# Tensor-engine experts without a loop, the last two experts interleaved, second-norm statistics on the scalar engine

## The reference, cut to what matters

```python
x1 = layer_norm(DEEPNORM_ALPHA * x + mix, ln1_g, ln1_b)
ffn = moe_ffn(x1, w_router, b_router, w_gate, b_gate, w_up, b_up, w_down, b_down)
x2 = layer_norm(DEEPNORM_ALPHA * x1 + ffn, ln2_g, ln2_b)

def expert_block(args):
    xe, e = args
    h = clamped_swiglu(xe @ w_gate[e] + b_gate[e], xe @ w_up[e] + b_up[e])
    return h @ w_down[e] + b_down[e]
```

## Time and profile before

| | us |
|---|---|
| Median of 3 runs (1635.64 to 1644.28) | 1637.16 |
| The profiled execution, whole time | 1636.67 |
| The profiled execution, span of the core | 1634.5 |
| PE busy in the span | 1492.2 |
| DVE, ACT, POOL busy | 388.5, 308.9, 113.5 |
| Mean traffic of the DMA engines | 287 GB/s |

### The profile page before, as it was taken

How to read it: one execution, slowest core, us unless ns; L and a number is a source line. 1 busy time by engine, 2 the same in 40 slices (tenths; PEclk the granted TensorE clock), 3 DMA queues, 4 the chain that set the end, 5 groups by cost and what they waited for, 6 DMA issues and landing times.

```text
span 1634.5 us, 38821 instructions
## 1 busy us (share of the span) xinstructions
PE 1492.2 (91%) x17456; PEld 1029.1 (63%) x17456; DVE 388.5 (24%) x620; ACT 308.9 (19%) x561; POOL 113.5 (7%) x123
## 2 busy tenths in 40 slices
PE   6999799887689989998998999899999989999991
PEld 6767697665656656665665666566566656666660
DVE  3422664535621111111111111111111111111104
ACT  4335332120121121111111111111111111121111
POOL 2002000000010000000001000000000000000000
PEclk8999555788589999999999999999999999999996
DMA  9322000032989999999999999999999999999923
GB/s 299 108 78 82 1 1 0 5 110 104 365 301 385 391 392 346 375 388 355 370 392 392 358 365 394 351 373 391 393 356 368 392 356 373 391 391 387 390 77 120
DMA packets 128644, 468.48 MB, mean 287 GB/s; under 512 B 11409, under 2 KB 12673, under 8 KB 128321
## 3 DMA queue, kind: packets, MB, share of 16 engines
q1 hardware_dynamic: 117648, 429.01, 67.9%
q0 software_dynamic: 10832, 36.89, 8.7%
HBM read 445.19 MB, written 22.76 MB: 286 GB/s over the span
## 4 chain that ended last, share of the span: by engine, by line
PE 82%; PEld 6%; issue 5%; DVE 4%; DMA 2%; ACT 1%; PEldq 0%; DVEq 0%; SPq 0%; ACTq 0%; POOLq 0%
PE unit L977 38%; PE unit L980 24%; PE unit L797 3%; PE unit L960 2%; PEld unit L632 2%; PEld unit L634 2%; PEld unit L633 2%; PE unit L965 2%; PE unit L994 2%; PE unit L761 1%; PE unit L784 1%; PE unit L632 1%; PE unit L930 1%; PE unit L633 1%; PE unit L634 1%
## 5 line engine op out<-in xcount | busy, mean ns | idle before, releaser
L980 PE MATMUL unit<-ring_a,xeT 128*32 128x256 f32 x1584 | 360.1, 387 | 0.0
L977 PE MATMUL unit<-ring_a,xeT 128*32 128x512 f32 (+1 forms) x3168 | 359.3, 496 | 0.0
L980 PE MATMUL unit<-ring_b,xeT 128*32 128x256 f32 x1488 | 329.1, 379 | 0.0
L977 PE MATMUL unit<-ring_b,xeT 128*32 128x256 f32 (+1 forms) x2976 | 328.2, 486 | 0.0
L980 PEld LDWEIGHTS unit<-ring_a,xeT 128*32 128x32 f32 x1584 | 176.5, 112 | 58.5 <-issue 4.5
L980 PEld LDWEIGHTS unit<-ring_b,xeT 128*32 128x32 f32 x1488 | 162.3, 110 | 52.6
L980 PE MATMUL unit<-ring_b,heT 128*32 128x256 f32 x816 | 181.0, 382 | 0.0
L977 PE MATMUL unit<-ring_b,heT 128*32 128x512 f32 (+1 forms) x1632 | 180.5, 490 | 0.0
L977 PEld LDWEIGHTS unit<-ring_a,xeT 128*32 128x32 f32 x3168 | 124.8, 112 | 72.5 <-issue 10.9
L980 PE MATMUL unit<-ring_a,heT 128*32 128x256 f32 x720 | 157.9, 379 | 0.0
L977 PE MATMUL unit<-ring_a,heT 128*32 128x256 f32 (+1 forms) x1440 | 157.5, 485 | 0.0
(11 more groups left out here) (292 smaller groups left out, 1620.3 us busy)
## 6 DMA issues: line engine op xcount, KB each, us to landing
ring_a<-w_gate_dram SPq DMA_DIRECT2D x68, 1024.0 KB, 9.0
ring_b<-w_down_dram SPq DMA_DIRECT2D x68, 1024.0 KB, 11.8
ring_a<-w_up_dram SPq DMA_DIRECT2D x64, 1024.0 KB, 10.9
ring_b<-w_up_dram SPq DMA_DIRECT2D x64, 1024.0 KB, 9.2
ring_b<-w_gate_dram SPq DMA_DIRECT2D x60, 1024.0 KB, 11.3
ring_a<-w_down_dram SPq DMA_DIRECT2D x60, 1024.0 KB, 10.4
raw_a<-w_in_dram SPq DMA_DIRECT2D x16, 512.0 KB, 4.8
raw_a<-w_out_dram SPq DMA_DIRECT2D x8, 512.0 KB, 3.4
```

The source lines that it names most:

```text
L977: return mm(out[j * NS:(j + 1) * NS, a:b], stat(j), w[:, a:b], start=False, stop=last)
L980: return mm(out[CAP:P, j * 256:(j + 1) * 256], stat(j), w[:, FOLD:D], start=False, stop=stop)
```

## The change

On PE the loop is gone: `pe_step` is written out for e from 0 to 30, and every wait for a chunk is against a constant. The other engines keep their loops.

For the last two experts PE's order is new. After the gate of expert 31 come up of 31, chunks 0 and 1 of down of 30, the transposes of h of 31, chunks 2 and 3 of down of 30, and down of 31 (`last_two`). SP requests the chunks in that order. The second h goes to a tile of its own, `heT_last`, which lies where the rows of even experts were, and the down product of 31 goes to `pg`. ACT copies h of 31 before it writes out expert 30. The numbers of instructions, chunks and bytes are those of before.

In the second norm DVE keeps the statistics of tile 0. Those of tiles 1 to 4 go to ACT: a pass that sums the row (Identity with an accumulator), the mean and its negative (two small Copies), a pass that sums the squares of the differences (Square with an accumulator), then the root. DVE then finishes one tile after the other.

```diff
 
         here[0] = phase_at
         xeT = sb("xeT", [P, 2, KD, CAP])
+        after_xeT = here[0]
+        here[0] = phase_at
+        heT_last = sb("heT_last", [P, FOLD // P, P])
+        here[0] = after_xeT
         heT = sb("heT", [P, FOLD // P, P])
         gm = sb("gm", [P, FOLD])
         sg = sb("sg", [P, FOLD])
...
         assert here[0] <= big_end
+        here[0] = phase_at
+        sq2 = sb("sq2", [P, D])
+        nm2 = sb("nm2", [P, NT])
         here[0] = raw_at
         raw_x = sb("raw_x", [P, KD, D])
...
@@ -469,11 +476,16 @@
                     weights(e, "w_up", 4 + PER * par, it)
                     weights(e + 1, "w_gate", 8 + PER * par, it)
                     weights(e, "w_down", 12 + PER * par, it)
-            for e in range(NE - TURN, NE):
+            for e in range(NE - TURN, NE - 2):
                 weights(e, "w_up", 4 + PER * e)
-                if e < NE - 1:
-                    weights(e + 1, "w_gate", 8 + PER * e)
-                weights(e, "w_down", (12 if e < NE - 1 else 8) + PER * e)
+                weights(e + 1, "w_gate", 8 + PER * e)
+                weights(e, "w_down", 12 + PER * e)
+            e = NE - 2
+            weights(e, "w_up", 4 + PER * e)
+            weights(e + 1, "w_gate", 8 + PER * e)
+            weights(e + 1, "w_up", 12 + PER * e)
+            weights(e, "w_down", 16 + PER * e)
+            weights(e + 1, "w_down", 20 + PER * e)
...
-            def h_of(k, j):
-                return heT[:, k, j * NS:(j + 1) * NS] if k < 6 else heT[:, 2 * j + k - 6, CAP:P]
+            def h_of(t):
+                return lambda k, j: t[:, k, j * NS:(j + 1) * NS] if k < 6 else t[:, 2 * j + k - 6, CAP:P]
...
-            def product(out, stat, which, sel, m0, chunks, it):
+            def product(out, stat, which, sel, m0, chunks):
 
                 if chunks[0] == 0:
                     biases(out, sel, bias[:, which])
                 for c in chunks:
                     m = m0 + c
-                    turns = (m // R2 + 1) if it is None else it * (TURN * PER // R2) + (m // R2 + 1)
-                    pe.wait_ge(w_in2[m % R2], turns * 16)
+                    pe.wait_ge(w_in2[m % R2], (m // R2 + 1) * 16)
                     for kk in range(2):
                         ins = tiles(out, lambda j: stat(2 * c + kk, j), ring[m % R2][:, kk], c == 3 and kk == 1)
                     ins.then_inc(slot_used, 1)
@@ -1020,44 +1031,53 @@
             pe.wait_ge(sel_ready, 1)
...
-            def pe_step(e, par, m0, it=None):
-
-                p2 = par % 2
-                last = isinstance(e, int) and e == NE - 1
-                no_more = isinstance(e, int) and e >= NE - 2
-                if not last:
-                    pe.wait_ge(x_rows, (e + 2) * 16)
-                    pe.wait_ge(he_ready, e + 1)
-                    x_T()
+            product(pg, x_of(0), 0, selr[:, 0], 0, range(4))
+
+            def pe_step(e, p2, m0):
+
+                no_more = e >= NE - 2
+                pe.wait_ge(x_rows, (e + 2) * 16)
+                pe.wait_ge(he_ready, e + 1)
+                x_T()
                 if not no_more:
                     pe.wait_ge(picked, e + 3)
                     pe.wait_ge(gate_read, e + 2)
                     rows_of(tok_done, CAP)
                 pe.wait_ge(h_ready, e + 1)
-                product(pu, x_of(p2), 1, selr[:, p2], m0, range(4), it)
-                if not last:
-                    pe.wait_ge(xe_ready, e + 2)
-                    pe.wait_ge(sel_ready, e + 2)
-                    pe.wait_ge(gate_read, e + 2)
-                    if not no_more:
-                        pe.wait_ge(idx_ready, e + 3)
-                    nxt = (pg, x_of(1 - p2), 0, selr[:, 1 - p2], m0 + 4)
-                    product(*nxt, range(3), it)
+                product(pu, x_of(p2), 1, selr[:, p2], m0, range(4))
+                pe.wait_ge(xe_ready, e + 2)
+                pe.wait_ge(sel_ready, e + 2)
+                pe.wait_ge(gate_read, e + 2)
+                if not no_more:
+                    pe.wait_ge(idx_ready, e + 3)
+                nxt = (pg, x_of(1 - p2), 0, selr[:, 1 - p2], m0 + 4)
+                product(*nxt, range(3))
                 pe.wait_ge(h_ready, e + 2)
                 h_T()
-                if not last:
-                    product(*nxt, range(3, 4), it)
+                product(*nxt, range(3, 4))
+                if no_more:
+                    last_two(e, p2, m0)
+                else:
+                    pe.wait_ge(he_ready, e + 2)
+                    pe.wait_ge(y_ready, e + 1)
+                    product(pd, h_of(heT), 2, selr[:, p2], m0 + 8, range(4))
+
+            def last_two(e, p2, m0):
+
+                product(pu, x_of(1 - p2), 1, selr[:, 1 - p2], m0 + 8, range(4))
                 pe.wait_ge(he_ready, e + 2)
                 pe.wait_ge(y_ready, e + 1)
-                product(pd, h_of, 2, selr[:, p2], m0 + (4 if last else 8), range(4), it)
-
-            with pe.Fori(0, NE // TURN - 1) as it:
-                for par in range(TURN):
-                    pe_step(it * TURN + par, par, 4 + PER * par, it)
-            for e in range(NE - TURN, NE):
-                pe_step(e, e % TURN, 4 + PER * e)
+                down = (pd, h_of(heT), 2, selr[:, p2], m0 + 12)
+                product(*down, range(2))
+                pe.wait_ge(h_ready, e + 3)
+                h_T()
+                product(*down, range(2, 4))
+                pe.wait_ge(he_ready, e + 3)
+                pe.wait_ge(gate_read, e + 3)
+                product(pg, h_of(heT_last), 2, selr[:, 1 - p2], m0 + 16, range(4))
+
+            for e in range(NE - 1):
+                pe_step(e, e % 2, 4 + PER * e)
 
 
...
@@ -1354,7 +1374,11 @@
             def sigmoid():
                 nc.scalar.activation(sg[:], gm[:], ACT.Sigmoid, scale=STEEP).then_inc(sig2, 1)
 
-            def y_out(e, par, m_end):
+            def h_in(e, t):
+                act.wait_ge(hT_done, e + 1)
+                copy(t[:].rearrange("p k s -> p (k s)"), px[:, 0:FOLD]).then_inc(he_ready, 1)
+
+            def y_out(e, par, m_end, pd=pd):
 
                 act.wait_ge(slot_used, m_end + R2)
...
             def act_step(e, par, it=None):
 
                 p2 = par % 2
-                act.wait_ge(hT_done, e + 1)
-                copy(heT[:].rearrange("p k s -> p (k s)"), px[:, 0:FOLD]).then_inc(he_ready, 1)
-                last = isinstance(e, int) and e == NE - 1
-                if not last:
-                    act.wait_ge(gate_read, e + 3)
-                    sigmoid()
-                y_out(e, p2, e * PER + (12 if last else 16))
-                if not (isinstance(e, int) and e >= NE - 2):
-                    n = e + 2
-                    if isinstance(n, int):
-                        pick_expert(eident[:, n:n + 1], p2)
-                    else:
-                        pick_expert(eident[:, bass.ds(n, 1)], p2)
-                    act.wait_ge(y_ready, n)
-                    rows_in(n, p2)
+                h_in(e, heT)
+                act.wait_ge(gate_read, e + 3)
+                sigmoid()
+                if isinstance(e, int) and e == NE - 2:
+                    h_in(e + 1, heT_last)
+                    y_out(e, p2, e * PER + 20)
+                    y_out(e + 1, 1 - p2, e * PER + 24, pg)
+                    return
+                y_out(e, p2, e * PER + 16)
+                n = e + 2
+                if isinstance(n, int):
+                    pick_expert(eident[:, n:n + 1], p2)
+                else:
+                    pick_expert(eident[:, bass.ds(n, 1)], p2)
+                act.wait_ge(y_ready, n)
+                rows_in(n, p2)
 
             with act.Fori(0, NE // TURN - 1) as it:
                 for par in range(TURN):
                     act_step(it * TURN + par, par, it)
-            for e in range(NE - TURN, NE):
+            for e in range(NE - TURN, NE - 1):
                 act_step(e, e % TURN)
...
             act.drain().then_inc(ended, 1)
 
             for i in range(NT):
-                r = rows(i)
-                act.wait_ge(var2, i + 1)
-                nc.scalar.activation(rs2[:r, i:i + 1], mv2[:r, i, 1:2], ACT.Sqrt, bias=EPS).then_inc(std2, 1)
+                r, x_ = rows(i), acc[:rows(i), i]
+                act.wait_ge(var2, 1)
+                if i:
+                    act.wait_ge(acc_back[i], 16)
+                    nc.scalar.activation(sq2[:r], x_, ACT.Identity, accum_out=mv2[:r, i, 0:1]).then_inc(stat2, 1)
+                    act.wait_ge(stat2, 3 * i - 2)
+                    nc.scalar.activation(mv2[:r, i, 0:1], mv2[:r, i, 0:1], ACT.Copy, scale=1.0 / D).then_inc(stat2, 1)
+                    act.wait_ge(stat2, 3 * i - 1)
+                    nc.scalar.activation(nm2[:r, i:i + 1], mv2[:r, i, 0:1], ACT.Copy, scale=-1.0).then_inc(nmean2, 1)
+                    act.wait_ge(nmean2, i)
+                    nc.scalar.activation(sq2[:r], x_, ACT.Square, bias=nm2[:r, i:i + 1], accum_out=mv2[:r, i, 1:2])\
```

(36 more changed lines are left out.)

## The result

The changed kernel took 1583.17 us in the median of 4 runs (1581.3 to 1589.82), the kernel before 1636.62 (4 runs). The ratio is 0.966, 95% interval 0.963 to 0.970. The forecast was 1585.6, with 1581 to 1597 as its range.

The account below looks back on a forecast made before the run. PE was taken to set the pace in the expert stage, with transfers following. Terms -43.0 + 1 - 6.0 + 1.3 - 4.4 = -51.1 us, from 1636.67, gave 1585.6 us, range 1581 to 1597.

Parts of the forecast that it names:

- Part 1, the jumps: PE's expert loop: writing it out removes six jumps back, 27.9 us of waiting and 15.1 of slow clock, -43.0 us.
- nothing was late next: Expert stage: the other engines still jump, but their jumps fall into idle time and were given no cost.
- The ring: Weight chunks: request-to-landing time grows 1.04 us per step to 39, just under 42.6 allowed; +1 us, from 0 to +6.
- The byte count: Weight transfers: by bytes alone, 12.58 MB used against 12.44 moved, landing time grows 0.4 us per step, to 21 us.
- Part 2, the last two: Experts 30 and 31: interleaved products shorten the stretch from 28.2 to 22.2 us, -6.0 us, from -5.7 to -6.1.
- The wait for the rows of 30: Write-out of expert 31: must wait until expert 30's rows are stored from the shared `ysb`; +1.3 us, 0 to +3.
- Part 3, the norm: Second norm: ACT's statistics take 3.1 us per tile and set the pace; -4.4 us, from -5.2 to -0.8.
- A: Rival, expert stage: weight transfers become the bound some steps before the end; 1592 to 1604 us, chance 0.10.
- B: Rival, second norm: Square and Sqrt need two table loads per tile, 6.0 us more; 1596 us, chance 0.07.
- C: Rival, expert stage: PE still pauses at the old places, waiting for another engine's jump; 1627.6 us, chance 0.03.
- D: Rival, expert stage: fetching PE's straight code behind the weight queue makes it slower; 1653 us at 0.6 per packet, chance 0.03.

Follow-up runs that it names:

- the ring of 8: The changed kernel with 8 places for weight chunks instead of 16: 1606.65 us. The kernel before, with 8 places: 1637.38 us.
- the ring of 12: The changed kernel with 12 places for weight chunks instead of 16: 1588.38 us.

## Why the prediction was right, point by point

- **Part 1, the jumps, -43.0:** -43.0 in the trace. Alone it gave 44.2 by the medians, 1.2 of it by a shorter slow clock in the last two experts. That nothing was late next held: the other engines' jumps cost nothing.
- **The ring, +1 (0 to 6):** 0. The slope of 1.04 us per step, taken from two kinds of chunks, was right to about a tenth: 0.93 up to step 12 by the ring of 8, 1.08 up to step 21 by the ring of 12. The lag at the end was 36 to 38 us where 39 was forecast. That it hardly grew behind step 24 was not foreseen, and why was not tested. The byte count (0.4 us per step) gave less than half of the slope because it rested on one step, the 12.44 MB of the earlier trace rows. With 12.28, the mean of the 29 steps, it gives (12.58 - 12.28) / 12.28 x 34.12 = 0.8 us per step, most of the slope. What the prediction also had wrong is where to look: it said that landing times would rise to 30 or 40 us. They stop at 18 to 25, because SP is held up and issues later.
- **Part 2, the last two, -6.0:** -5.9 against the kernel before, alone and in the changed kernel; -4.75 against the kernel with PE written out alone, where the slow clock was shorter.
- **The wait for the rows of 30, +1.3 (0 to +3):** 0. The failing step is the landing time of the addition, taken as 8.6 us beside weights. The last weights had landed at 1547.6, 1.5 us before it was issued, and it landed after 5.6 us, so 3.4 + 5.6 = 9.0 us lay under a product of 10.7. Beside weights, as in the kernel with PE written out alone, the addition of 30 did take 9.1 us.
- **Part 3, the norm, -4.4 (-5.2 to -0.8):** -4.7, with 3.01 us per tile where 3.1 were taken. Three terms are off and nearly cancel. A wait of ACT on itself costs 0.02 to 0.04 us, not 0.05. The root adds 0.10 us, not 0.20, since the next tile's first pass starts 0.10 us behind its start. The Square pass with the read of its accumulator takes 1.24 us, where the sum took 1.14 for each pass.
- **Sum:** -51.1 forecast from 1636.67; -53.7 between the events, with 1.0 of the difference in the ring, 1.3 in the wait and 0.3 in the norm. So the terms are right to 1.3 us each. The median, 2.4 us below the forecast, can't confirm that, since the mixer alone moves a run by more.
- **The rivals:** A did not come, but it was near: with four places fewer the ring costs 7.5 us, with eight fewer 16. B: no load between Square and Sqrt. C and D: no stop at any step, and the pieces of code cost nothing beside a queue that was full for 1000 us. The Trainium skill, "Runtime: NRT & Kernel Launch", "Instruction fetch mechanics", says that a taken branch whose target lies outside the prefetched window stalls the fetch, and that the fetch of straight code is mostly hidden. This trace agrees, with 4.65 us of waiting per jump and 0 per straight step. That PE stands for the fetch at a jump is not shown by any run: the trace has only "issue" there.

## What to carry to other kernels

Price a hardware loop on PE by its jumps: read the stop and the slower step behind it from the trace (here 4.7 + 2.5 us each), and multiply by the turns less one. Before taking out pauses of the engine that sets the pace, ask what recovers in them: here the transfers did, and with a ring of 8 places the same edit gives 16 us less. A part worth a few us is to be read between two events of the trace when the whole time spreads over 10.

## What the runs showed of the hardware that was not expected

- A stop of PE as short as 1.9 us brought a stretch at lower granted clock (0.79 in the mean of 8 us) and cost another 1.6 us. The price was uneven at 3.0 us of standing, from 0.0 to 3.0 us at one place or another, and even again at 4.2 (2.7 to 2.9).
- SP's issue of 1 MB transfers was held up with about eight of them under way, though the places in the ring were free. From there the time from issue to landing stays between 18 and 25 us and no longer shows how far the transfers are behind. What holds SP up is not shown.
- The mixer, the same in all kernels, took up to 11 us more in some profiled executions than in others (step 1 at 501.5 to 512.4 us). In the two compared above, the longer one had more of it at 1.2 GHz. What decides it was not studied.
